# One GpSimd instruction per weight chunk in the mixers, and sums over one element for two kinds of VectorE copies

## The chip, the cores and the metric

The kernel runs on one core of a Trainium2 chip. The metric is the device time of one execution in microseconds (us). The core has TensorE (matrix products, here written PE; PEld is its weight load), VectorE (DVE), ScalarE (ACT), GpSimd (POOL) and SyncE (SP), which here only issues DMAs. They run side by side and meet in semaphores.

## The reference

Two small networks of two layers each run one behind the other on a batch of 256 rows of 1024 columns, all in float32:

```python
def first_block(x, ...):
    for layer in range(2):
        h = rmsnorm(x, norm_mix_g[layer])
        mix = retention_nsa_mixer(h, ...) if layer == 0 else hgrn2_mixer(h, ...)
        x = x + mix
        h = rmsnorm(x, norm_ffn_g[layer])
        x = x + (silu(h @ w1) * (h @ w3)) @ w2
    return rmsnorm(x, final_norm_g)

def second_block(x, ...):            # layer norm, ALPHA = 4 ** 0.25
    for l in range(2):
        mix = diff_attention(x, ...) if l == 0 else chunk_attention(x, ...)
        x = layer_norm(ALPHA * x + mix)
        x = layer_norm(ALPHA * x + (silu(x @ gate) * (x @ up)) @ out)
    return x
```

The first mixer holds a retention of 4 heads and an attention of 8 heads in three branches (compressed, selected, window), each with its own softmax and a gate. For the compressed branch the keys and values, 32 rows at a time, have position embeddings added and go through a small gelu network. The second mixer (HGRN) is a recurrence with forget gates, worked out as products whose decays are cumulative sums; the part close to the diagonal is built level by level (blocks of 64, 32, 16 down to 1 rows). The third is a differential attention, the fourth a chunked attention with a position bias.

## The kernel before

**Stages.** There are 8: 0, 2, 4, 6 are the mixers, 1, 3, 5, 7 the gated feed-forward parts. All weights, 403 blocks ("chunks") of mostly 128 x 1024 float32, are streamed from HBM once, in the order of use.

**Split products.** A float32 product is made of three fast ones: each operand is split in a high part (the value rounded to the fast format) and a low part (the rest), and high x high, low x high and high x low are summed. For a weight chunk c, SyncE loads `raw[c % 4]` (it waits until the low part of chunk c - 4 is done), ScalarE copies it to `whi[c % 6]` in the rounded format (L2028; it waits until TensorE is done with chunk c - 6), and GpSimd subtracts, `wlo = raw - whi` (L2328). TensorE uses whi at L1048 and L1049, wlo at L1055 (L1074 and L1077 in the feed-forward parts, where the weights are the moving operand the other way round). GpSimd does hardly anything else. It makes the low part of a chunk in pieces and signals after the last: pieces of 256 columns for the mixers' chunks from c = 8 on and for the first six chunks of each feed-forward stage, one of up to 1024 columns for the others.

**Order of work.** A unit is one chunk times 128 rows of activations. The plan, a table written out by hand for each stage, says behind which unit which side steps stand; each engine walks through the same table in its own order and issues only the steps it has. So an engine works strictly in its written order, and a step that waits holds all steps behind it on that engine. Weight splits (whi, wlo) stand behind the units that free their buffers.

**Steps around the change**, with their names in the plan:
- MB, `place_positions` (VectorE, stage 0): puts the 16 position columns for keys and values beside the data, Z <- CP (L1577), two copies of 128 x 16. Behind it VectorE's next step is CB.
- CB, CE, CD, CF (stage 0): the gelu of the compression. CB has a product x * x of two SBUF tiles (L1536), CE is ScalarE's exponential, CD ends with L1553, and TensorE's CF is L1166 and L1169. GD is two scalar steps on the gates (L1567), GE ScalarE's sigmoid of them (L2017, L2019, L2021).
- NW, `norm_weights` (stage 0): for each of the 12 softmaxes a reciprocal (L1661), before it in four of them a scalar step on the sums (L1659), then a product with the gates, SM <- SM of 4 columns (L1663), and the weights, W <- A,SM (L1671). TensorE's TR (L1215) turns W.
- DB, `diagonal_blocks` (stage 2): four copies of 32 x 128 from DG to the diagonal of MX (L1923), four times in the stage. TensorE's O1 reads MX. Behind the first DB in VectorE's order stands FF, which makes the logarithm of the forget gates (L1833 to L1838); ScalarE's FG (L2238) waits for it, and behind that come EV (L2041) and TA, the copy of the turned heads into QK (L2253), for which TensorE's H1 (L1315) waits.
- AP of stage 3 (L1455): X <- X,SM,LC, four of 128 x 512, the last norm of the first network. XT turns X on TensorE.

DG and MX, Z and CP, and SM are SBUF tiles; A and G are PSUM.

Of the kernel before, what the change touches and what calls it, by code (L numbers as in the profile page):

```python
# [9 lines left out]
ALU = mybir.AluOpType  # L10
ACT = mybir.ActivationFunctionType
X_AX = mybir.AxisListType.X
# [133 lines left out]
NR, NH = 4, 6  # L146
# [65 lines left out]
CHUNK_STAGE = {u.chunk: u.st for u in UNITS}  # L212
# [11 lines left out]
FIRST = [UNITS[BEGIN[st]].chunk for st in range(8)]  # L224
# [498 lines left out]
def program(nc, a, out):  # L723
    ctx = ExitStack()
    with ctx:
        def sb(name, shape, dt=F, stack=ctx):
            return stack.enter_context(nc.sbuf_tensor(name, shape, dt))
# [20 lines left out]
        CP = sb("CP", [128, NCOLP], F, above)  # L748
# [15 lines left out]
        Z = sb("Z", [128, 6, 256], F, e0)  # L764
# [32 lines left out]
        rows = sb("rows", [128, 256], F, ffn)  # L797
# [40 lines left out]
        def nth(kind, *key):  # L838

            return TURN[kind, key]  # L840

        def heads4(ap, n):
            return ap.rearrange("p (h k) -> p h k", h=n)
# [554 lines left out]
        def _(e):  # L1398
# [6 lines left out]
            def own():  # L1405

                e.wait_ge(s_dve, dv.n)
# [163 lines left out]
            def place_positions(key):  # L1571
                e.wait_ge(d_id, 16)
                e.wait_ge(d_cp, 16)
                e.memset(Z[:, 2:6:3, :], 0.0).then_inc(s_dve, dv.up())
                own()
                for kind, at_pos in enumerate((POSK, POSV)):
                    m = e.tensor_copy(Z[:, 3 * kind + 2, 0:32:2], CP[:, at_pos:at_pos + 16])  # L1577
                m.then_inc(S["MB"], 1)

            def mask_scores(key):  # L1580
# [333 lines left out]
            def diagonal_blocks(key):  # L1914

                _, u = key
                mixed = MX[:, :, 256 * u:256 * u + 256].rearrange("p t (i c) -> p t i c", i=2)
                blocks = DG[:, 4 * (u % 2):4 * (u % 2) + 4, :].rearrange("p (i t) c -> p t i c", t=2)
                e.wait_ge(S["H5"], max(nth("H5", 2, 2 * u + i, t) for i in range(2) for t in range(2)))
                e.wait_ge(S["HA"], max(nth("HA", 2, 2 * u + i, t) for i in range(2) for t in range(2)))  # L1920
                for j in range(4):
                    rows = slice(32 * j, 32 * j + 32)
                    m = e.tensor_copy(mixed[rows, :, :, rows], blocks[rows])  # L1923
                m.then_inc(S["DB"], 1)

            def hgrn_gate(key):
# [49 lines left out]
            def first_lo(key):  # L1976
# [5 lines left out]
                     "HW": turned_hidden_lo, "XL": x_lo, "BN": layer_stats,  # L1982
                     "AG": layer_aggregate, "AP": apply_norm, "HM": gate_times_up, "HL": hidden_lo, "ML": mixed_lo,
                     "CB": gelu_argument, "CD": gelu_done, "CG": compress_copy, "GD": gates_clamp, "MK": mask_scores, "MB": place_positions,
                     "RC": invert_sums, "CB2": diff_combine, "CPV": copy_weights, "NW": norm_weights, "NO": branch_sum, "NA": branches_added, "WL": turned_lo, "RO": rotate,
                     "R2V": ret_copy, "R4": ret_decay, "R6": ret_stats, "R8": ret_gate, "GS": ret_gate_clamp,
                     "B1": bound_begin, "B3": bound_ready, "FB": forget_clamp, "FD": forget_bound,
                     "FF": forget_log, "FJ": forget_done, "GB": gate_clamp, "GF": gate_done, "TV": heads_copy,
                     "H3": decay_heads, "H5": sum_levels, "DB": diagonal_blocks, "O3": hgrn_gate, "KV": k_copy, "NF": diff_norm,
                     "P1": lam_products, "P3": lam_ready}  # L1990
            for st in range(8):
# [328 lines left out]
        @block.gpsimd  # L2320
        def _(e):
            def lo(c):
                n = STREAM[c][2]
                short = CHUNK_STAGE[c] % 2 == 0 and c >= 8 or CHUNK_STAGE[c] % 2 and c < FIRST[CHUNK_STAGE[c]] + NH
                cuts = list(range(0, n, 256 if short else 1024)) + [n]
                e.wait_ge(s_hi, c + 1)
                for i, j in zip(cuts, cuts[1:]):
                    m = e.tensor_tensor(wlo[c % NH][:, i:j], raw[c % NR][:, i:j], whi[c % NH][:, i:j].bitcast(F),  # L2328
                                        ALU.subtract)
                m.then_inc(s_lo, 1)  # L2330

            def bias_mask(key):
                _, p = key
                tb = heads4(TB[p % 2][:, :], 4)
                km = CN[:, C_KM:C_KM + 256].unsqueeze(1).to_broadcast([128, 4, 256])
                e.wait_ge(d_tb[p % 2], 16 * (p // 2 + 1))
                e.tensor_tensor(tb, tb, km, ALU.add).then_inc(S["TBM"], 1)

            e.wait_ge(s_lo, 1)
            for c in SPLIT_AT[-1][1:]:  # L2340
                lo(c)
            for st in range(8):
                for u in range(-1, BEGIN[st + 1] - BEGIN[st]):
                    for kind, key in PLACE.get((st, u), ()):
                        if kind == "TBM":
                            bias_mask(key)
                    for c in SPLIT_AT.get(BEGIN[st] + u + 1, ()) if u >= 0 else ():
                        lo(c)
# [46 lines left out]
```

## Time and profile before

| | |
|---|---|
| median of 3 runs | 1274.83 us (1274.36 to 1276.19) |
| the profiled execution | 1274.34 us |
| its span, first to last instruction | 1272.5 us |
| TensorE busy | 1256.7 us, 99% |
| GpSimd busy | 1029.1 us, 81% |
| ScalarE busy | 766.1 us, 60% |
| VectorE busy | 501.2 us, 39% |
| granted TensorE clock | 0.999 of full speed |

A busy TensorE is one whose pipelined products overlap; their ends are modelled. In the timeline a line holds instructions of one kind that follow each other, and its time runs from the start of the first to the end of the last.

### The profile page before, as it was taken

What the parts mean: (1) busy time and instruction counts of PE and PEld (TensorE: products, weight loads), DVE (VectorE), ACT (ScalarE), POOL (GpSimd) and SP (SyncE); (2) the same over time, 40 slices, a digit from 0 to 9 for tenths busy, and PEclk for the clock granted to TensorE, in tenths of its full rate; (3) what the DMA queues carried; (4) which work ended last, traced back from release to release, by engine and by line L of the source; (5) the groups of instructions that cost most, each with busy time, mean ns of one, the idle gap of its engine ahead of it and who ended that gap; (6) DMA issues with size and microseconds to landing.
All of it is one profiled execution on the core that took longest, in us unless ns stands there. A gap on an engine that the chain in (4) does not pass through costs nothing.

```text
span 1272.5 us, 20336 instructions
## 1 busy us (share of the span) xinstructions
PE 1256.7 (99%) x7562; PEld 1055.9 (83%) x7562; DVE 501.2 (39%) x1108; ACT 766.1 (60%) x1481; POOL 1029.1 (81%) x874
## 2 busy tenths in 40 slices
PE   8999999999999999999999999999999999999997
PEld 7877888888887887888888888888888888888886
DVE  3575423331168862333105665133203345233302
ACT  7656676654688877666445685365534565366631
POOL 6666789878977568988888877798889887699874
PEclk9999999999999999999999999999999999999999
DMA  8543566656654436666666545677565644567652
GB/s 284 159 133 108 158 209 217 194 166 185 183 163 134 134 94 206 195 187 189 178 194 195 162 150 148 198 213 218 184 196 174 224 149 136 162 215 224 202 171 82
DMA packets 63121, 224.96 MB, mean 177 GB/s; under 512 B 7344, under 2 KB 7984, under 8 KB 63024
## 3 DMA queue, kind: packets, MB, share of 16 engines
q1 hardware_dynamic: 62736, 223.57, 57.1%
q8 instruction: 60, 0.98, 0.3%
q14 instruction: 37, 0.30, 0.1%
q10 hardware_dynamic: 288, 0.10, 0.0%
HBM read 222.59 MB, written 1.05 MB: 176 GB/s over the span
## 4 chain that ended last, share of the span: by engine, by line
PE 94%; DVE 2%; POOL 2%; ACT 2%; DMA 1%; issue 1%; SPq 0%; DVEq 0%; ACTq 0%
PE G L1048 18%; PE G L1049 17%; PE G L1055 17%; PE G L1074 10%; PE A L1074 10%; PE A L1077 5%; PE G L1077 5%; POOL wlo L2328 1%; PE A L1179 1%; PE A L1103 1%; PE A L1215 1%; PE A L1239 1%; DMA X<-in_x 0%; PE A L1339 0%; PE A L1318 0%
## 5 line engine op out<-in xcount | busy, mean ns | idle before, releaser
L2328 POOL TENSOR_TENSOR wlo<-raw,whi 128x256 fp32r<-128x256 f32 (+2 forms) x866 | 1019.6, 1213 | 225.8 <-ACT whi L2028 224.8
L2028 ACT ACTIVATE whi<-raw 128x1024 fp32r<-128x1024 f32 x403 | 422.3, 1057 | 199.6 <-PE G L1055 145.0
L1048 PE MATMUL G<-whi,xx 128*128 128x512 f32 (+1 forms) x560 | 226.0, 404 | 0.5 <-DVE xx L1435 0.3
L1049 PE MATMUL G<-whi,xx 128*128 128x512 f32 (+1 forms) x560 | 217.1, 388 | 0.0
L1055 PE MATMUL G<-wlo,xx 128*128 128x512 f32 (+1 forms) x560 | 171.3, 388 | 0.0
L1074 PE MATMUL G<-xx,whi 128*128 128x512 f32 x576 | 144.7, 393 | 0.0
L1074 PE MATMUL A<-xx,whi 128*128 128x512 f32 x576 | 144.4, 393 | 0.0
L1048 PE MATMUL G<-whi,hh 128*128 128x512 f32 x352 | 137.6, 391 | 0.0
L1049 PE MATMUL G<-whi,hl 128*128 128x512 f32 x352 | 137.2, 390 | 0.0
L1048 PEld LDWEIGHTS G<-whi,xx 128*128 128x128 f32 x560 | 105.3, 188 | 24.9 <-issue 5.5
L1055 PEld LDWEIGHTS G<-wlo,xx 128*128 128x128 f32 x560 | 104.6, 188 | 22.4
L1049 PEld LDWEIGHTS G<-whi,xx 128*128 128x128 f32 x560 | 105.6, 189 | 17.9
L1074 PEld LDWEIGHTS A<-xx,whi 128*128 128x128 f32 x576 | 103.9, 189 | 18.7
L1074 PEld LDWEIGHTS G<-xx,whi 128*128 128x128 f32 x576 | 103.7, 189 | 18.4
L1055 PE MATMUL G<-wlo,hh 128*128 128x512 f32 x352 | 108.5, 390 | 0.0
L1077 PEld LDWEIGHTS G<-xx,wlo 128*128 128x128 f32 x576 | 78.6, 191 | 5.6
L1077 PEld LDWEIGHTS A<-xx,wlo 128*128 128x128 f32 x576 | 78.6, 191 | 5.6
L1077 PE MATMUL A<-xx,wlo 128*128 128x256 f32 x576 | 80.4, 283 | 0.0
L1077 PE MATMUL G<-xx,wlo 128*128 128x256 f32 x576 | 80.4, 283 | 0.0
L1055 PEld LDWEIGHTS G<-wlo,hh 128*128 128x128 f32 x352 | 66.1, 188 | 13.8
L1048 PEld LDWEIGHTS G<-whi,hh 128*128 128x128 f32 x352 | 66.1, 188 | 13.4
L1049 PEld LDWEIGHTS G<-whi,hl 128*128 128x128 f32 x352 | 66.1, 188 | 13.4
(388 smaller groups left out, 1499.3 us busy)
## 6 DMA issues: line engine op xcount, KB each, us to landing
raw<-in_g SPq DMA_DIRECT2D x88, 512.0 KB, 3.9
raw<-in_u SPq DMA_DIRECT2D x88, 512.0 KB, 4.1
raw<-in_d SPq DMA_DIRECT2D x88, 512.0 KB, 4.0
raw<-in_w_h SPq DMA_DIRECT2D x32, 512.0 KB, 3.6
raw<-in_w_e SPq DMA_DIRECT2D x24, 512.0 KB, 3.9
raw<-in_w_a SPq DMA_DIRECT2D x24, 512.0 KB, 3.6
raw<-in_w_b SPq DMA_DIRECT2D x24, 512.0 KB, 3.7
raw<-in_w_eo SPq DMA_DIRECT2D x8, 512.0 KB, 3.6
```

The source lines that it names most:

```text
L1048: e.matmul(o, sh[:, kt, xs], whi[h][:, ws], start=u.first and j == 0, stop=False)
L1049: e.matmul(o, sl[:, kt, xs], whi[h][:, ws], start=False, stop=False)
L1055: m = e.matmul(o, sh[:, kt, xs], wlo[h][:, ws], start=False, stop=u.stop and final)
L1074: e.matmul(o[:, :], whi[h][:, 128 * kt:128 * kt + 128], xx[:, kt, :], start=kt == 0, stop=False)
L1077: m = e.matmul(o[:, 0:256], wlo[h][:, 128 * kt:128 * kt + 128], xx[:, kt, 0:256], start=False, stop=kt == u.kts[-1])
L1103: m = e.transpose(A[t][:, 512 * b + 128 * i:512 * b + 128 * i + 128], X[:, t, 512 * b + 128 * i:512 * b + 128 * i + 128], ident)
L1179: m = e.matmul(tile[:, at:at + nk], qs[i], ks[i], start=True, stop=True, skip_group_check=True)
L1215: m = e.transpose(tile[0:kp, (i * nb + b) * 128:(i * nb + b) * 128 + 128], s[:, 2 * i if key[0] == 4 else i, 128 * b:128 * b + kp], ident)
L1239: m = e.matmul(heads4(tile[64 * g:64 * g + 64, 0:256], 2), v, wt[:, g:4:2, b, :], start=b == 0, stop=b == nb - 1, skip_group_check=True)
L2028: e.activation(whi[c % NH][:, 0:n], raw[c % NR][:, 0:n], ACT.Copy).then_inc(s_hi, 1)
L2328: m = e.tensor_tensor(wlo[c % NH][:, i:j], raw[c % NR][:, i:j], whi[c % NH][:, i:j].bitcast(F), ALU.subtract)
```

## The change

```diff
@@ place_positions
                 for kind, at_pos in enumerate((POSK, POSV)):
-                    m = e.tensor_copy(Z[:, 3 * kind + 2, 0:32:2], CP[:, at_pos:at_pos + 16])
+                    m = e.tensor_reduce(Z[:, 3 * kind + 2, 0:32:2], CP[:, at_pos:at_pos + 16].unsqueeze(2), X_AX, ALU.add)
                 m.then_inc(S["MB"], 1)
@@ diagonal_blocks
                 for j in range(4):
                     rows = slice(32 * j, 32 * j + 32)
-                    m = e.tensor_copy(mixed[rows, :, :, rows], blocks[rows])
+                    m = e.tensor_reduce(mixed[rows, :, :, rows], blocks[rows].unsqueeze(4), X_AX, ALU.add)
                 m.then_inc(S["DB"], 1)
@@ gpsimd, lo(c)
                 n = STREAM[c][2]
-                short = CHUNK_STAGE[c] % 2 == 0 and c >= 8 or CHUNK_STAGE[c] % 2 and c < FIRST[CHUNK_STAGE[c]] + NH
+                short = CHUNK_STAGE[c] % 2 and c < FIRST[CHUNK_STAGE[c]] + NH
                 cuts = list(range(0, n, 256 if short else 1024)) + [n]
```

All mixers' chunks now get their low part in one GpSimd instruction. The copies of the position columns and of the diagonal blocks become VectorE sums over an added axis of length one, with the same result. No wait, signal or order changes.

## Rows read from the trace of the kernel before

**Rows 1.** The page's first part: busy us (share of the span) xinstructions.
```profile
PE 1256.7 (99%) x7562; PEld 1055.9 (83%) x7562; DVE 501.2 (39%) x1108; ACT 766.1 (60%) x1481; POOL 1029.1 (81%) x874
```

**Rows 2.** Groups by form, GpSimd: shapes xcount | busy us, mean ns | idle before, releaser.
```profile
L2328 POOL TENSOR_TENSOR wlo<-raw,whi 128x1024 fp32r<-128x1024 f32 x247 | 587.4, 2403 | 105.8 <-ACT whi L2028 105.1
L2328 POOL TENSOR_TENSOR wlo<-raw,whi 128x256 fp32r<-128x256 f32 x616 | 431.5, 740 | 120.0 <-ACT whi L2028 119.7
```

**Rows 3.** Waits of TensorE: engine line waited for: total us, times, longest.
```profile
PE A L1315 <- ACT QK L2253: 1.7, 1, 1.7
...
PE A L1124 <- DVE PJ L1869: 0.3, 1, 0.3
```

**Rows 4.** Groups by form, VectorE: the two kinds of copies.
```profile
L1923 DVE COPY MX<-DG 32x128 f32<-32x128 f32 x16 | 10.4, 648 | 0.2
...
L1577 DVE COPY Z<-CP 128x16 f32<-128x16 f32 x2 | 4.8, 2428 | 0.0
```

**Rows 5.** Timeline, VectorE, stage 2: start us, us, engine line op, tiles, xcount [idle before].
```profile
391.68 5.00 DVE L1923 COPY MX<-DG 32x128 f32<-32x128 f32 x4
396.71 0.69 DVE L1833 SCALAR_TENSOR_TENSOR W<-PJ,G 128x512 f32<-128x512 f32 x1
...
429.02 0.90 DVE L1923 COPY MX<-DG 32x128 f32<-32x128 f32 x4
```

**Rows 6.** Timeline, ScalarE, stage 2.
```profile
392.78 0.60 ACT L2227 ACTIVATE G<-W 128x512 f32<-128x512 f32 x1
...
399.55 1.20 ACT L2238 ACTIVATE lf<-G 64x512 fp32r<-64x512 f32 x2 [1.46 <-DVE PJ L1838]
```

**Rows 7.** Windows: us, PE, PEld, DVE, ACT, POOL busy (x), clock, DMA share, GB/s.
```profile
960.00:976.00 16.00, 15.72 (x78) 12.65 (x77) 10.95 (x17) 7.02 (x13) 16.00 (x24) 1.00 0.61 175
```

**Rows 8.** Timeline, GpSimd, three unbroken runs of stage 0.
```profile
38.79 13.91 POOL L2328 TENSOR_TENSOR wlo<-raw,whi 128x256 fp32r<-128x256 f32 x20 [1.28 <-ACT whi L2028]
60.57 11.10 POOL L2328 TENSOR_TENSOR wlo<-raw,whi 128x256 fp32r<-128x256 f32 x16 [7.87 <-ACT whi L2028]
...
102.43 5.60 POOL L2328 TENSOR_TENSOR wlo<-raw,whi 128x256 fp32r<-128x256 f32 x8 [2.88 <-ACT whi L2028]
```

**Rows 9.** Timeline, VectorE, stage 0.
```profile
39.59 0.67 DVE L1536 TENSOR_TENSOR G<-W 64x30 f32<-64x30 f32 x1
...
44.21 0.18 DVE L1553 TENSOR_TENSOR W<-A,W 64x30 f32<-64x30 f32 x1
...
48.95 1.00 DVE L1567 TENSOR_SCALAR SM<-PJ 128x24 f32<-128x24 f32 x2
...
51.38 0.65 DVE L1663 TENSOR_TENSOR SM<-SM 128x4 f32<-128x4 f32 x1
...
53.07 0.16 DVE L1663 TENSOR_TENSOR SM<-SM 128x4 f32<-128x4 f32 x1
...
65.67 0.53 DVE L1659 TENSOR_SCALAR SM<-SM 128x4 f32<-128x4 f32 x1
...
66.45 0.43 DVE L1663 TENSOR_TENSOR SM<-SM 128x4 f32<-128x4 f32 x1
...
103.31 0.58 DVE L1659 TENSOR_SCALAR SM<-SM 128x4 f32<-128x4 f32 x1
```

**Rows 10.** Timeline, TensorE, the steps of stage 0 that read those results.
```profile
45.36 0.39 PE L1169 MATMUL A<-w2c,W 64*15 64x64 f32 x4
...
52.80 0.65 PE L1215 MATMUL A<-CN,W 128*128 128x128 f32 x4
...
67.85 0.61 PE L1215 MATMUL A<-CN,W 128*15 128x128 f32 x4
...
106.00 0.60 PE L1215 MATMUL G<-CN,W 128*15 128x128 f32 x4
```

**Rows 11.** Timeline, ScalarE, the first step of the gates' sigmoid.
```profile
50.25 0.26 ACT L2017 ACTIVATE SM<-SM 128x48 f32<-128x48 f32 x1
```

**Rows 12.** Timeline, VectorE, a pair of normalised rows at the start of stage 4.
```profile
675.38 1.90 DVE L1455 SCALAR_TENSOR_TENSOR X<-X,SM,LC 128x512 f32<-128x512 f32 x2 [0.88 <-ACT SM L2013]
```

## The prediction

> **What bounds the kernel now.** I read the engines' busy times first. TensorE is busy 1256.7 us, 99% of the span, GpSimd 81%, VectorE 39% [rows 1]. So nothing is gained by less work on GpSimd or VectorE as such; an edit counts where TensorE stands still today, and where it would begin to stand still. Second, the waits of TensorE. Behind the start-up they are few: 1.7 us in one place for ScalarE's copy into QK and 0.3 us for VectorE's gate product, both in the third stage (HGRN) [rows 3]; in the table of windows, the one around the start of the last mixer lacks 0.28 us of 16 [rows 7]. Third, GpSimd by form: a 1024-column subtraction takes 2403 ns, one of 256 columns 740 ns [rows 2]; run back to back, four of them take some 2.8 us (11.10 us for 16) [rows 8]. Fourth, and it decides here, VectorE's timeline beside GpSimd's. Some VectorE instructions wait for whatever GpSimd is running. A 4-column product of two SBUF tiles takes 0.16 us with GpSimd idle and 0.65, 0.43 us beside it [rows 9]; four copies of 32x128 take 0.90 us together with GpSimd idle, 5.00 us beside it [rows 5]; two 16-column copies beside the 1024-column form take 2428 ns each, one whole GpSimd instruction [rows 4]. The price of a meeting is thus what is left of the running GpSimd instruction: up to 0.74 us now, up to 2.40 us after the change. By the Trainium skill (SBUF — State Buffer, Who interferes with whom), a 2-port copy, or a VectorE instruction with two SBUF inputs, and a GpSimd one exclude each other for the whole instruction, and a tensor_reduce never takes part; by that rule, the trace agrees.
>
> **The change part by part.**
>
> *GpSimd.* 131 chunks of the four mixers (27 of stage 0, 40 + 32 + 32 of the others) go from four pieces to one instruction: 520 of the 616 pieces of 256 columns go (the other 96 are those of the odd stages), and three small ones. A chunk becomes ready 2.80 - 2.40 = 0.4 us sooner, some 50 us less of GpSimd's time in all, and that time was hidden behind TensorE. What it brings: SyncE refills each raw buffer 0.4 us sooner, and where GpSimd runs without a break ScalarE's next high part follows. The one place where TensorE lacks time near such an unbroken run is that window at the start of the last mixer; I take its whole 0.28 us (bounds 0 and 0.28).
>
> *Sums for copies.* The 16 copies of blocks and the 2 of positions no longer wait. A sum over one element is not in the trace. Bounds for one of 32x128: 0.22 us, the copy beside an idle GpSimd (0.90 for four [rows 5]), and 0.65 us, the mean of today's copies [rows 4]. I take 0.28, nearer to the idle copy, as it streams the same 128 columns; four are 1.1 us. The two copies of positions save some 4.5 us of VectorE (4.8 less two short sums [rows 4]); nothing stands behind them there, so 0, bounds 0 and 0. Of the blocks, one group matters. It ends at 391.68 + 5.00 = 396.68, and the forget-gate chain begins behind it at 396.71 [rows 5], though its input has lain ready since 392.78 + 0.60 = 393.38; its last result is what ScalarE waits 1.46 us for at 399.55 [rows 6]. With sums VectorE is free at 392.8, the chain moves up by 3.3 us, ScalarE never waits, and its next copies, those that TensorE waits 1.7 us for, are 1.46 us earlier: 1.46 gained (bounds 1.46 and, were a sum as dear as today's mean, 4 x 0.65 = 2.6, still 1.46). The last group of blocks stands before the gate chain that TensorE waits 0.3 us for [rows 3]: 0.3 gained, bounds 0 and 0.3. Together 0.28 + 1.46 + 0.3 = 2.04 us gained.
>
> *What is late next.* The sums are only exempt themselves. In stage 0 the softmaxes keep their products of two 4-column SBUF tiles (12 of them, L1663) and scalar steps on them (4, L1659), the compression two products (L1536), the gates two scalar steps (L1567). I replay GpSimd's runs with 2.40 us per chunk [rows 8], whose high parts lie ready, and follow VectorE to the next TensorE instruction that needs the result.
> - Run of 38.79, five chunks. The product at 39.59 is held until 41.19, ends 1.0 us later than now, and the second one behind it meets the next chunk's instruction (41.19 to 43.6) and ends 1.35 late. The result that ended at 44.21 + 0.18 = 44.39 [rows 9] ends at 45.74; TensorE takes it at 45.36 [rows 10]: 0.45 lost with its 0.07 of handing over (bounds 0 and 1.35).
> - Same run. ScalarE's third high part is queued behind that second product's exponential, so the last three chunks run at 45.6, 48.0 and 50.4 to 52.8. The two scalar steps of 48.95 stand at 49.4: the first waits for 50.4, the second for 52.8, where both end at 49.95 now. ScalarE's sigmoid of the gates, which started at 50.25 [rows 11], starts at 52.95, 2.25 late beyond the shift. The product of 51.38 then finds GpSimd idle, 0.16 for 0.65 [rows 9]. TensorE's step of 52.80 [rows 10] is 2.25 - 0.49 = 1.8 later (bounds 0 and 2.25).
> - Run of 60.57: instructions start at 60.57, 62.97, 65.37, 67.77. The scalar step of 65.67 is held to 67.77, the reciprocal follows, and the product, at 68.1 instead of 66.45, meets the fourth and ends at 70.25 for 66.88 [rows 9]: 3.4 late. The weights would have been ready at 67.14 and TensorE takes them at 67.85 [rows 10]: 3.4 - 0.7 = 2.7 lost (bounds 0 and 3.4).
> - Run of 102.43: the same pair at 103.31 [rows 9] is held to 104.83 and, at 105.15, to 107.23, 2.7 late; TensorE takes the weights at 106.00 [rows 10], 1.15 after they are ready now: 1.55 lost (bounds 0 and 2.7).
> - The other eight products fall into gaps of GpSimd or have over 1 us to spare: 0. The normalised rows at the start of stage 4, one pair of which takes 1.90 us beside GpSimd [rows 12], can be held by one instruction, 2.4 us; I see room for most of it and take 0 (bounds 0 and 2.4). VectorE's lambda steps there: 0, nobody waits for them soon.
> Sum: 0.45 + 1.8 + 2.7 + 1.55 = 6.5 us lost, all on TensorE's path.
>
> One rule of the skill speaks against this sum. Advanced Engine Details and Errata (VectorE Performance Modes, Mode Summary) names only 2-port instructions as interfering with GpSimd. The product of two SBUF tiles would then never wait; it gives the fourth rival.
>
> Net: 6.5 - 2.0 = 4.5, rounded down to 4.4, as a TensorE that stands gives the others time. The profiled execution took 1274.34 us, the median run 1274.83; 1274.34 + 4.4 = 1278.7, and on the median's side 1279.2.
>
> **The rivals.**
> 1. *Only the gains show* (the other side). A TensorE stall lets high parts and GpSimd drift, and the held steps fall into gaps; the 0.4 us per chunk is passed on through refills. Place and price: the wait for QK's copy in the HGRN stage, 1.7 us whole, the two others, 0.6, and the 0.5 us by which the product of 51.38 is shorter: 2.8, so 1272.0. It decides if the steps of 65.67 and 103.31 both miss a GpSimd instruction. For it: eight of twelve products meet none that matters; against: both stand in the middle of an unbroken run.
> 2. *One of the pairs meets, the rest doesn't*: 2.7 + 0.45 - 2.0 = 1.1, or without the first 0.45, 0.7; about 1275.7, no change. For it: every hit depends on phases of a microsecond.
> 3. *Held longer than one instruction.* The first copy of 391.68 was passed over by several pieces: the four took 5.00, not 4 x 0.74 = 3.0 [rows 5]. If each of two pairs, and the rows of stage 4, lose another 2.4, it is 4.4 + 5 = 9.4: 1284.2.
> 4. *Only copies and scalar steps wait.* Then 0 at the first place, 1.8 at the second; at 65.67 only the first of the pair waits, 1.4 late, 0.7 lost; nothing at 103.31: 2.5 - 2.0 = 0.5, 1275.3. Against: the product's 0.65 and 0.43 beside 0.16 [rows 9].
> 5. *The sums wait too.* Then blocks cost up to 4 x 2.4 = 9.6 for 5.00, 4.6 more at a place without slack: 1274.8 + 6.5 + 4.6 = 1285.9.
>
> **How the numbers follow.** Forecast 0.50, rivals 0.12, 0.18, 0.12, 0.05, 0.03. What the measurement tells from no change is about 0.2%, 2.5 us. Slower: 0.50 + 0.12 + 0.03, and a little of it is lost to the middle: 0.64. Same: 0.18 + 0.05 + 0.01: 0.24. Faster: 0.12. The range runs from 1272.8 (most of the first rival left out) to 1284.0. The forecast's own range is 1276.5 to 1282.
>
> **What would show it.** Right: 474 GpSimd instructions instead of 866, busy some 70 us less than 1029.1 us (128 x (4 x 0.74 - 2.40)); sums at 0.2 to 0.35 us each, unheld; no 1.46 us wait of ScalarE near 400; L1663 and L1659 with single durations of 1.5 to 2.4 us; TensorE waits of 1 to 3 us before the weight transposes (L1215) in the first 110 us. Wrong: no instruction of L1659 or L1663 above 1 us, or such ones with TensorE's transposes unmoved (then slack was larger than read); sums of 0.6 us or more beside GpSimd; a stage 0 as long as before.

## The result and the profile after

The changed kernel took 1279.78 us, median of 5 runs (1278.67 to 1281.59); the kernel before, five runs beside it, 1274.83 us. The ratio is 1.0036, its interval 1.0025 to 1.0047: slower by about 0.36%. The prediction was 1279.2 us. The profiled execution took 1278.67 us against 1274.34 us, its span 1276.8 against 1272.5: 4.3 us more, where 4.4 were predicted.

First the page's first part, after, to set beside [rows 1].

```profile
PE 1257.7 (99%) x7562; PEld 1055.4 (83%) x7562; DVE 504.3 (39%) x1108; ACT 766.3 (60%) x1481; POOL 973.4 (76%) x482
```

TensorE has 1.0 us more of work in it and 3.3 us more of standing. GpSimd lost 392 instructions and 55.7 us, and the time did not follow. By form, the kernel after (shapes, count, busy us, mean ns, idle before), GpSimd and then VectorE, to set beside [rows 2, 4]:

```profile
L2328 POOL TENSOR_TENSOR wlo<-raw,whi 128x1024 fp32r<-128x1024 f32 x375 | 891.5, 2404 | 270.0 <-ACT whi L2028 269.3
L2328 POOL TENSOR_TENSOR wlo<-raw,whi 128x256 fp32r<-128x256 f32 x96 | 67.2, 744 | 15.7 <-ACT whi L2028 15.7
```

```profile
L1663 DVE TENSOR_TENSOR SM<-SM 128x4 f32<-128x4 f32 x12 | 7.2, 602 | 0.4
L1455 DVE SCALAR_TENSOR_TENSOR X<-X,SM,LC 128x512 f32<-128x512 f32 x4 | 7.1, 1811 | 2.6 <-ACT SM L2013 2.6
L1923 DVE TENSOR_REDUCE MX<-DG 32x128 f32<-32x128 f32 x16 | 4.4, 275 | 0.2
L1659 DVE TENSOR_SCALAR SM<-SM 128x4 f32<-128x4 f32 x4 | 3.9, 970 | 0.0
```

The sum over one element costs 275 ns, where the prediction took 280. Then the waits of TensorE after (engine, line, what it waited for, us in total, times, longest):

```profile
PE A L1215 <- DVE W L1671: 2.8, 2, 2.4
...
PE A L1103 <- DVE X L1455: 1.8, 2, 1.1
PE G L1215 <- DVE W L1671: 1.3, 1, 1.3
...
PE A L1169 <- DVE W L1553: 0.2, 1, 0.2
```

None of these four stood there before, and both lines of [rows 3] are gone. The softmax weights of stage 0 (L1215) and the gelu's result (L1169) were forecast; the normalised rows of stage 4 (L1103) were in the bounds but not in the sum. Now VectorE's timeline of the kernel after, to set beside [rows 9, 5, 12] in that order; start and duration in us:

```profile
39.63 1.64 DVE L1536 TENSOR_TENSOR G<-W 64x30 f32<-64x30 f32 x1
...
42.31 1.30 DVE L1536 TENSOR_TENSOR A<-W 64x30 f32<-64x30 f32 x1
...
49.30 1.06 DVE L1567 TENSOR_SCALAR SM<-PJ 128x24 f32<-128x24 f32 x2
...
51.73 0.91 DVE L1663 TENSOR_TENSOR SM<-SM 128x4 f32<-128x4 f32 x1
...
66.30 2.02 DVE L1659 TENSOR_SCALAR SM<-SM 128x4 f32<-128x4 f32 x1
68.35 0.18 DVE L1661 RECIPROCAL SM<-SM 128x4 f32<-128x4 f32 x1
68.56 2.04 DVE L1663 TENSOR_TENSOR SM<-SM 128x4 f32<-128x4 f32 x1
...
106.43 1.54 DVE L1659 TENSOR_SCALAR SM<-SM 128x4 f32<-128x4 f32 x1
...
108.22 2.07 DVE L1663 TENSOR_TENSOR SM<-SM 128x4 f32<-128x4 f32 x1
...
396.32 1.14 DVE L1923 TENSOR_REDUCE MX<-DG 32x128 f32<-32x128 f32 x4
398.05 0.69 DVE L1833 SCALAR_TENSOR_TENSOR W<-PJ,G 128x512 f32<-128x512 f32 x1 [0.59 <-ACT G L2227]
...
677.71 5.67 DVE L1455 SCALAR_TENSOR_TENSOR X<-X,SM,LC 128x512 f32<-128x512 f32 x2 [0.88 <-ACT SM L2013]
```

The product of four columns takes 0.16 us when nothing holds it; here it takes 2.04 and 2.07. GpSimd's timeline after, beside [rows 8], shows what holds it:

```profile
38.85 4.70 POOL L2328 TENSOR_TENSOR wlo<-raw,whi 128x1024 fp32r<-128x1024 f32 x2 [1.71 <-ACT whi L2028]
45.52 7.10 POOL L2328 TENSOR_TENSOR wlo<-raw,whi 128x1024 fp32r<-128x1024 f32 x3 [1.97 <-ACT whi L2028]
...
63.56 7.03 POOL L2328 TENSOR_TENSOR wlo<-raw,whi 128x1024 fp32r<-128x1024 f32 x3
...
105.55 4.72 POOL L2328 TENSOR_TENSOR wlo<-raw,whi 128x1024 fp32r<-128x1024 f32 x2 [3.72 <-ACT whi L2028]
```

The three instructions from 63.56, the last of four that run without a break, end at 70.59 and VectorE's product ends at 70.60; the two from 105.55 run to 110.27 and the other product ends at 110.29. TensorE's steps behind them, beside [rows 10], and the window of [rows 7]:

```profile
45.72 0.39 PE L1169 MATMUL A<-w2c,W 64*15 64x64 f32 x4 [0.25 <-DVE W L1553]
...
53.42 0.33 PE L1215 MATMUL A<-CN,W 128*128 128x128 f32 x1 [0.39 <-DVE W L1671]
...
70.92 0.61 PE L1215 MATMUL A<-CN,W 128*15 128x128 f32 x4 [2.37 <-DVE W L1671]
...
110.60 0.61 PE L1215 MATMUL G<-CN,W 128*15 128x128 f32 x4 [1.32 <-DVE W L1671]
```

```profile
960.00:976.00 16.00, 16.00 (x76) 13.26 (x75) 7.81 (x13) 8.39 (x13) 15.88 (x8) 1.00 0.62 191
```

Subtract before from after, and each start from the next, and the losses stand there: 45.72 - 45.36 = 0.36; 53.42 - 52.80 = 0.62, 0.26 more; 70.92 - 67.85 = 3.07, 2.45 more; 110.60 - 106.00 = 4.60, 1.53 more. I did the same for every matmul of the program, the nth of one trace against the nth of the other. Below, a "step" is a place where this lag jumps; its place is told by the time in the kernel before.

### The profile page after: what moved, and what is told of

It reads as the page before. It is cut to its first block, busy times and chain, and to the rows that moved or that the text cites. A ratio compares the mean times of both kernels' runs of the same rounds, so it can differ in the third digit from the quotient of the medians.

```text
span 1276.8 us, 19944 instructions
## 1 busy us (share of the span) xinstructions
PE 1257.7 (99%) x7562; PEld 1055.4 (83%) x7562; DVE 504.3 (39%) x1108; ACT 766.3 (60%) x1481; POOL 973.4 (76%) x482
## 4 chain that ended last, share of the span: by engine, by line
PE 94%; DVE 3%; ACT 1%; issue 1%; DMA 0%; SPq 0%; DVEq 0%; ACTq 0%
PE G L1048 18%; PE G L1049 17%; PE G L1055 17%; PE G L1074 10%; PE A L1074 10%; PE G L1077 5%; PE A L1077 5%; PE A L1179 1%; PE A L1103 1%; PE A L1215 1%; DMA X<-in_x 0%; PE A L1339 0%; PE A L1239 0%; PE A L1318 0%; PE A L1379 0%
## 5 line engine op out<-in xcount | busy, mean ns | idle before, releaser
L2328 POOL TENSOR_TENSOR wlo<-raw,whi 128x1024 fp32r<-128x1024 f32 (+2 forms) x474 | 963.9, 2064 | 285.8 <-ACT whi L2028 285.0
```

## The experiments

The theory: the new losses are VectorE instructions held by GpSimd's longer one at four places of stage 0 and, since the result, at one of stage 4. The rivals: the sums themselves cost something; the single instructions delay loads or high parts; or the losses come from elsewhere and only happen to end at those places.

The kernel before was timed again beside the experiments: median 1274.32 us (22 runs) beside the first four, 1275.92 us (26 runs) beside the last four. So the ratios are to be compared, and the times only within one of the two sets.

**The sums alone.** The kernel before, with both sums and its four pieces.

```diff
-                    m = e.tensor_copy(mixed[rows, :, :, rows], blocks[rows])
+                    m = e.tensor_reduce(mixed[rows, :, :, rows], blocks[rows].unsqueeze(4), X_AX, ALU.add)
...
```

Only one of the two sums is shown; the other is the same in `place_positions`.

> The kernel before with both kinds of copies as sums, GpSimd still in four pieces. Theory (sums take VectorE out of GpSimd's way, single instructions are what costs): the ScalarE wait of 1.46 us near 400 goes, the gate chain at 468 comes 0.6 earlier: 2.2 us faster than before, 1272.6. Rival (the gain at these places came from the single instruction, which leaves GpSimd idle more often): same as before, 1274.8. Each sum 0.26 to 0.28 us, beside GpSimd or not.

Measured 1272.36 us (11 runs), ratio 0.9983 (0.9974 to 0.9992). VectorE's timeline of this kernel, around the first group of blocks:

```profile
391.44 1.14 DVE L1923 TENSOR_REDUCE MX<-DG 32x128 f32<-32x128 f32 x4
393.17 0.69 DVE L1833 SCALAR_TENSOR_TENSOR W<-PJ,G 128x512 f32<-128x512 f32 x1 [0.59 <-ACT G L2227]
```

The four take 1.14 us where the copies took 5.00 [rows 5], and the chain behind them starts at 393.17, not 396.71. TensorE's lag steps by -1.59 at 404.52, where its 1.7 us wait stood, and by -0.50 at 468.17. So the sums are a gain, beside four pieces as well, and not the cause of the loss.

**The single instruction alone.** The change with the copies kept.

```diff
-                    m = e.tensor_reduce(mixed[rows, :, :, rows], blocks[rows].unsqueeze(4), X_AX, ALU.add)
+                    m = e.tensor_copy(mixed[rows, :, :, rows], blocks[rows])
...
```

> The kernel before with one GpSimd instruction per mixer chunk and the copies kept. Theory: all losses of the changed kernel (0.36 + 0.27 + 2.44 + 1.53 in stage 0, 2.4 at the start of stage 4, some 7.0) without its gains, and the copies are held by up to 2.4 us each: the group at 391.68 has no slack behind it, so TensorE's wait there (1.7 us before) grows by 0 to 4.6; 1274.8 + 7.0 - 0.4 = 1281.4 at least, 1286 at most. Rival (copies get in between two chunks and cost no more than beside the pieces, as GpSimd is idle more): 1281.4 to 1282 with the wait unchanged. Rival (the losses come from the sums): about 1273, faster than before.

Measured 1280.76 us (1279.75 to 1283.30, 5 runs), ratio 1.0057 (1.0043 to 1.0071). The steps of stage 0 are those of the changed kernel: 0.31, 0.25, 2.43 and 1.48. But the first group of blocks went another way than expected (this kernel's timeline of VectorE):

```profile
395.92 1.49 DVE L1923 COPY MX<-DG 32x128 f32<-32x128 f32 x4
397.65 0.69 DVE L1833 SCALAR_TENSOR_TENSOR W<-PJ,G 128x512 f32<-128x512 f32 x1 [0.24 <-ACT G L2227]
```

The copies were hardly held, the first for 0.6 us and the others not at all: GpSimd was through with its instruction at 396.64 and had no next one until 398.67, the expectation's first rival. TensorE gained 1.59 us at 404.52 without any sum. The long wait for QK's copy thus goes with either half of the change, and the two gains do not add. At the last group the copies are held still: this kernel's waits of TensorE have `PE A L1124 <- DVE PJ L1869` with 0.6 us, which the sums take away.

**Four pieces again in stage 0**, all else as changed.

```diff
-                short = CHUNK_STAGE[c] % 2 and c < FIRST[CHUNK_STAGE[c]] + NH
+                short = CHUNK_STAGE[c] % 2 and c < FIRST[CHUNK_STAGE[c]] + NH or CHUNK_STAGE[c] == 0 and c >= 8
```

> The changed kernel with four pieces per chunk in stage 0 again. Theory (VectorE held in stage 0): the four steps back there are gone, 0.36 + 0.27 + 2.44 + 1.53 = 4.6 us less than the changed kernel; the 2.4 of stage 4 stay: 1279.8 - 4.6 = 1275.2. Rival (delays are taken back by what TensorE's waiting gives the other engines, so that undoing them returns only part): 1277 to 1279.

Measured 1274.59 us (11 runs), ratio 1.0001 (0.9992 to 1.0010). All steps of stage 0 are gone, 4.6 us; the loss that is left is stage 4's, and the gains make up for it.

```profile
672.79 5.68 DVE L1455 SCALAR_TENSOR_TENSOR X<-X,SM,LC 128x512 f32<-128x512 f32 x2 [0.88 <-ACT SM L2013]
```

**Four pieces for the first eight chunks of stage 4**, all else as changed.

```diff
+                short = ... or CHUNK_STAGE[c] == 4 and c < FIRST[4] + 8
```

> The changed kernel with four pieces for the first 8 chunks of stage 4 only, those beside the normalised rows (L1455). Theory: TensorE's two waits for L1455 (1.18 + 0.97) and the 0.27 behind go: 2.4 us less than the changed kernel, 1277.4; L1455 back to at most 1.2 us. Rival (L1455 was late by chance of that one profile): 1279.8, the same as the changed kernel.

```profile
680.47 1.90 DVE L1455 SCALAR_TENSOR_TENSOR X<-X,SM,LC 128x512 f32<-128x512 f32 x2 [0.88 <-ACT SM L2013]
```

The pair is back at its 1.90 us of [rows 12], and the steps of 1.28, 0.97 and 0.19 at 677 to 680 us, 2.4 together, are gone. The time, 1277.85 us (1276.15 to 1281.14, 6 runs), ratio 1.0028 (1.0017 to 1.0040), is 1.9 below the changed kernel's, with a wide spread of which the last section tells.

**The held steps themselves, another form.** All else as changed, the products of L1663 and the steps of L1659 are made one column at a time, each with one SBUF column and a scalar.

```diff
...
-                    e.tensor_tensor(gr[key], rs[key], gates[:, at:at + 4], ALU.mult).then_inc(s_dve, dv.up())
+                    for i in range(4):
+                        m = e.tensor_scalar(gr[key][:, i:i + 1], rs[key][:, i:i + 1], gates[:, at + i:at + i + 1], None,
+                                            ALU.mult)
+                    m.then_inc(s_dve, dv.up())
```

> The changed kernel with the 12 products (L1663) and the 4 scalar steps (L1659) of the softmaxes split in four steps of one column each, with the factor as a scalar operand. In the trace of before, scalar steps of one column beside GpSimd took 0.15 us (L1974). Theory (these instructions are held because they read SBUF the way GpSimd does; the length of GpSimd's instruction harms only them): TensorE's waits of 2.44 and 1.53 us at the weight transposes go and nothing else moves: 1278.7 - 4.0 = 1274.7, and no spread of 3 us between runs. Rival (the single instruction delays the low parts or the loads, and VectorE only shows it): 1278 to 1280 as before, plus the added steps, 0.3 us each.

Measured 1274.90 us (11 runs), ratio 0.9996 (0.9987 to 1.0005). VectorE's timeline of this kernel; by its GpSimd timeline four 1024-column instructions run from 60.79 to 70.20 without a break:

```profile
65.87 0.33 DVE L1660 TENSOR_SCALAR SM<-SM 128x1 f32<-128x1 f32 x4
66.22 0.18 DVE L1663 RECIPROCAL SM<-SM 128x4 f32<-128x4 f32 x1
66.44 0.57 DVE L1666 TENSOR_SCALAR SM<-SM 128x1 f32<-128x1 f32 x4
```

Eight steps and the reciprocal end in 1.14 us where the two steps of four columns and theirs took 4.3, at the same place, with GpSimd's instructions as long as ever. TensorE's steps at 67.85 and 106.00 are gone; those at 45.36 (L1536, 0.31) and in stage 4 stay. This is the sharpest of the tests: at these two places the long instruction harms only through the form of VectorE's step. Late loads or high parts would have stayed.

**Pieces in both stages.** The conditions of the third and fourth experiment together.

> The changed kernel with pieces in stage 0 and for the first 8 chunks of stage 4. Theory (the two places are all that costs and they add up): 1274.6 (pieces in stage 0) - 2.4 = 1272.2, as fast as the sums alone (1272.4) or 0.3 better. Rival (the single instruction has a cost everywhere that the two places do not show): slower than the sums alone by 0.5 or more.

Measured 1271.74 us (1271.50 to 1272.37, 6 runs), ratio 0.9972 (0.9961 to 0.9984): faster than the kernel before by 0.28%. All of the lag's steps behind the start-up are now gains: -1.59 at 404.52, -0.34 at 454.38, -0.50 at 468.17, and -0.26 at 971.95, the window of [rows 7]. Most of this is the sums' work: alone they made 0.17%, and the two intervals overlap (0.9974 to 0.9992 and 0.9961 to 0.9984). In the profiles the span is 1270.0 us here and 1270.3 us with the sums alone, so merging the other chunks gives some 0.3 us by these two profiles (the step at 454.38 is missing with the sums alone), which the times don't tell apart from nothing.

**Two pieces of 512 in all mixers.**

```diff
-                cuts = list(range(0, n, 256 if short else 1024)) + [n]
+                cuts = list(range(0, n, 256 if short else 512 if CHUNK_STAGE[c] % 2 == 0 and c >= 8 else 1024)) + [n]
```

> The changed kernel with two pieces of 512 columns per chunk in all mixers. Theory (an instruction is held for what is left of the running piece, here up to 1.25 us): the pair of 66 loses 2 x 1.2 less what it lost before, some 1.4 for a slack of 0.7, so 0.7 instead of 2.44; the pair of 106 0.9 late for 1.15 of slack, 0; stage 4 up to 1.0; with the sums' 2.2: 1274.3 + 0.7 + 0.5 + 0.3 - 2.2 = 1273.6. Rival (proportional to the length without slack): half of the losses of 7.0, 1275.6.

Measured 1272.59 us (10 runs), ratio 0.9975 (0.9966 to 0.9984). Its VectorE timeline has the third length of the same hold:

```profile
65.61 1.23 DVE L1659 TENSOR_SCALAR SM<-SM 128x4 f32<-128x4 f32 x1
66.88 0.18 DVE L1661 RECIPROCAL SM<-SM 128x4 f32<-128x4 f32 x1
67.09 0.98 DVE L1663 TENSOR_TENSOR SM<-SM 128x4 f32<-128x4 f32 x1
```

The pair takes 0.96 us beside pieces of 256 columns (0.53 + 0.43 [rows 9]), 2.21 beside 512, 4.06 beside 1024; TensorE's step at 67.85 is 0, 0.59 and 2.44 us. Of the pair's added 1.25 and 3.10 us 0.66 were slack each time, near the 0.7 of the prediction, and the rest is lost. The time is 1.0 us below the theory's 1273.6: 0.6 of this pair's 0.7 came, but of what it allowed for the other places only 0.1 at 52.80 did, and stage 4 lost nothing.

**One-column steps, and pieces only where other steps are held.** Pieces for the chunks 8 to 16 (L1536, L1567) and the first eight of stage 4, one instruction elsewhere.

```diff
+                short = ... or 8 <= c < 17 or CHUNK_STAGE[c] == 4 and c < FIRST[4] + 8
```

> Single columns for the softmaxes' products and scalar steps, four pieces for chunks 8 to 16 of stage 0 (compression and gates) and for the first 8 of stage 4, one instruction elsewhere, sums. Theory: no VectorE instruction is held anywhere where TensorE has no slack, also not by 0.4 to 0.5 us beside pieces: the 0.28 at 52.8 goes too: 1272.2 - 0.2 = 1272.0, the fastest. Rival (the added steps cost VectorE more than the waits did): 1272.4 to 1273.

Measured 1272.07 us (1271.82 to 1274.47, 10 runs), ratio 0.9976 (0.9966 to 0.9985). It is not told apart from the version with pieces in both stages: once no step on TensorE's path is held, neither way is worth more than the other.

## Why the prediction was right

The sum was right, 4.3 for 4.4 in the profiled execution, and so was the kind of cause: VectorE steps held for what is left of GpSimd's instruction, and TensorE waiting for them. That the number came within 0.1 us is luck. One loss was taken 1.5 too large, another 2.4 too small, and the gains some 0.8 too small: 7.0 lost and 2.9 gained, where 6.5 and 2.04 were written.

- *The first run (L1536): 0.45 predicted, 0.36 measured.* The product ends at 39.63 + 1.64 = 41.27, for 41.19 + handing over, and the second meets the next instruction, as written.
- *The gates' scalar steps (L1567): 1.8 predicted, 0.27 measured.* This term was mis-sized. GpSimd's second run came as forecast (45.52 to 52.62, for 45.6 to 52.8) and the first scalar step was held, as forecast. But the pair ended after 1.06 us: the second slipped in behind the first, where one GpSimd instruction gave way to the next, and ScalarE's sigmoid began at 50.61, not at 52.95. A loss is left because the product of 51.73, which was to find GpSimd idle, was now early enough to be held to the run's end, 0.91 us.
- *The pair of 65.67: 2.7 predicted, 2.44 measured. The pair of 103.31: 1.55 predicted, 1.53 measured.* Here a reciprocal stands between the two held steps, and each time the second found the next GpSimd instruction begun. It does not follow that steps back to back always go together: in the kernel before, the two scalar steps of 48.95 took 0.30 and 0.78 us, the second held for a whole piece of its own, and the rows of stage 4 below were held twice, back to back. What decides whether a second step slips in is not shown.
- *Stage 4 (L1455): 0 predicted with the bound 2.4, 2.4 measured.* The two rows take 5.67 us for 1.90, 3.8 more. TensorE takes them here, in the kernel before and then in the changed one:

```profile
677.11 0.60 PE L1103 MATMUL A<-CN,X 128*128 128x128 f32 x4
...
678.93 0.60 PE L1103 MATMUL A<-CN,X 128*128 128x128 f32 x4
```

```profile
680.64 0.66 PE L1103 MATMUL A<-CN,X 128*128 128x128 f32 x4 [1.07 <-DVE X L1455]
```

In the kernel before the rows end at 676.14 and 677.28, 1.0 and 1.65 us before TensorE takes them. The prediction wrote "I see room for most of it"; there was room for 1.3 of the 3.8. It had followed VectorE to the next TensorE instruction at the places of stage 0, and not here. It had also counted one hold, and each of the two rows met one (2.88 and 2.87 us); that its bound of 2.4 was just reached is chance. GpSimd was held in turn, as it seems by the first row, which ran until 680.59: of the changed kernel's three instructions below, the last, from 680.00, took 2.83 us for 2.40.

```profile
675.29 7.54 POOL L2328 TENSOR_TENSOR wlo<-raw,whi 128x1024 fp32r<-128x1024 f32 x3
```

- *The wait for QK's copy: 1.46 predicted, 1.59 measured. The gate chain: 0.3 and 0.50. The window of the last mixer: 0.28 and 0.52*, its TensorE column now 16.00. Another 0.27 came at 454.38 (L1339), where TensorE stood 1.2 us before and 0.9 us after; the prediction had no term for it. The mechanism given for the first was right for the sums alone; the single instruction alone takes the wait away too. The credit to the sums in the changed kernel was thus too large at this place: what they add to the single instruction is the difference at the last group, 0.32 lost with copies, 0.50 gained with sums.
- *GpSimd's busy time: 70 less predicted in the last part, 55.7 measured.* The sum there used the mean duration, 740 ns, where the part on GpSimd had some 50 from the 2.8 us of four back to back; instructions back to back overlap, and 431.5 us / 616 = 700 ns of engine time each [rows 2]. For the 128 full chunks that is 128 x (4 x 0.700 - 2.404) = 51. It touched no time.

Of the rivals, the gains alone and one pair alone did not happen, as both pairs met an instruction; held longer than one instruction did not happen either, as every held product ended with the instruction that was running when it began, and each row of stage 4 met one. The rule of the Trainium skill (Advanced Engine Details and Errata, VectorE Performance Modes, Mode Summary), read alone, would leave the product of two SBUF tiles alone; its 2.04 us refute that. The other statement of the Trainium skill (SBUF — State Buffer, Who interferes with whom), that two SBUF inputs are enough and that a tensor_reduce never contends, agrees with it and with the 275 ns of a sum: 7 of the 16 lay wholly beside a running GpSimd instruction, and none took over 0.28 us.

## What to carry to other kernels

Making an engine's instructions longer is free only as far as nobody on the path shares something with it for the length of one instruction. Before merging such instructions, list every instruction of the other engine that was ever held (its duration in the timeline far above the same form's elsewhere), and follow each one to the next step of the busiest engine, at the places that look harmless too. And if a hold is found, change the held step's form or shorten the other engine's instructions only there: here another form at two places gave back 4 us of the 7, and shorter instructions at the held places, with either form, all of it. Then ask what the merging itself is worth: the kernel was 0.28% faster than before, but the sums alone made 0.17% of it.

## What the runs showed of the hardware

**A stand of TensorE was followed once by a lower clock.** In the profile of the kernel with four pieces in stage 4 alone, TensorE stood 2.39 us before L1215 at 70.78, as in the changed kernel, and then the granted clock fell. The table of windows of that kernel (us, then PE, PEld, DVE, ACT, POOL busy, clock, DMA share, GB/s):

```profile
68.00:70.80 2.80, 0.41 (x9) 0.22 (x6) 2.70 (x5) 0.00 (x0) 2.44 (x2) 1.00 0.78 249
70.80:72.00 1.20, 1.20 (x8) 0.86 (x10) 1.17 (x3) 0.56 (x1) 0.00 (x0) 0.68 0.69 181
72.00:73.00 1.00, 1.00 (x8) 0.61 (x4) 0.38 (x1) 0.61 (x4) 0.00 (x0) 0.50 0.76 238
...
76.00:78.00 2.00, 2.00 (x10) 1.25 (x10) 0.80 (x1) 1.17 (x5) 0.00 (x0) 0.50 0.00 0
78.00:80.00 2.00, 2.00 (x14) 1.57 (x11) 1.55 (x4) 0.91 (x5) 0.00 (x0) 0.98 0.00 0
```

From full (2.4 GHz) it goes to half (1.2 GHz) for more than 6 us, and TensorE's lag grows there from 2.9 to 5.9 us. In the changed kernel's profile the same window holds the same stand and the clock stays:

```profile
68.00:70.80 2.80, 0.55 (x8) 0.35 (x8) 2.70 (x5) 0.00 (x0) 2.58 (x2) 1.00 0.75 253
70.80:72.00 1.20, 1.08 (x10) 0.80 (x11) 1.17 (x4) 0.44 (x1) 0.00 (x0) 1.00 0.60 174
```

In the profile with the copies kept the clock stays too. So the price of such a stand differs between executions, 2.4 us or some 5.4. It fits the times: the changed kernel's runs fall in two groups, 1278.67 to 1279.78 and 1281.54 to 1281.59 us, those with copies kept in 1279.75 to 1280.76 and 1283.10 to 1283.30, those of the kernel of this profile in 1276.15 to 1276.64 and 1279.06 to 1281.14; the six kernels without the stand spread by at most 1.3 us but for a single run of the last experiment. That the upper group is this fall was seen in one profile only; elsewhere it is not shown. Lower group against lower group, the pieces in stage 4 gave back 2.7 us, and not the 1.9 of the medians. The prediction's 4.4 us is the lower group; the median stands 5.0 us above the kernel before.

The kernel before has two groups as well, though it has no stand before L1215: of its 53 runs 32 took 1274.06 to 1275.30 us and 21 took 1275.73 to 1277.02 us. All six kernels above lack its 1.7 us wait for QK's copy, and none has a second group, only that single run. Whether that wait costs the clock in some executions is open, as no profile fell in its upper group. It bears on the ratios: beside the last four experiments 15 of its 26 runs were in the upper group, and against the lower one (median 1274.70 us) pieces in both stages are 0.23% faster.

**One column is not held.** A VectorE step of one column with a scalar took 0.14 to 0.22 us; 29 of the 64 lay wholly within a running GpSimd instruction. One of four columns, the same operation on the same tile, took 2.02. Four such steps, 0.33 or 0.57 us together, are therefore cheaper than one that is held that long. The Trainium skill's condition for the 2-port mode (Advanced Engine Details and Errata, VectorE Performance Modes, 2x-2p Requirements), an even or equal odd count above one, would leave one column out; by that rule, the trace agrees.
